# Sample's attention: one buffer of transposed rows with waits per piece, and five buffers of gathered rows instead of four

## The reference, cut to what matters

```python
def mla_sample(q_lat, q_pe, ckv_new, kpe_new, pool_ckv, pool_kpe, page_table):
    DB, T, H, C = q_lat.shape
    ckv_past = pool_ckv[page_table].reshape(DB, -1, KV_LORA)
    kpe_past = pool_kpe[page_table].reshape(DB, -1, MLA_ROPE)
    s_past = jnp.einsum('bqhc,bkc->bhqk', q_lat, ckv_past) + jnp.einsum('bqhr,bkr->bhqk', q_pe, kpe_past)
    ...
    p = jax.nn.softmax(s, axis=-1).astype(ckv_new.dtype)
    return (jnp.einsum('bhqk,bkc->bqhc', p[..., :P], ckv_past)
            + jnp.einsum('bhqk,bkc->bqhc', p[..., P:], ckv_new))
```

## Time and profile before

| what | value |
|---|---|
| median of three runs | 2132.25 us (2132.25 to 2144.01) |
| profiled execution | 2130.03 us, its span 2128.3 us |
| mean granted TensorE clock | 0.981 |
| PE, DVE, ACT, POOL busy in the span | 94%, 68%, 36%, 13% |
| the stage of the change | from 821.4 us (first transpose) to about 1341 us |

### The profile page before, as it was taken

The page is one execution under the profiler, slowest core; times in us unless marked ns, Lnnn a source line. Parts: engine busy times, 40 slices in busy tenths (PEclk is TensorE's granted clock), DMA queues, the critical chain, the costliest instruction groups (busy, mean ns, idle before and its releaser), DMA issues. The chain is left out here.

```text
span 2128.3 us, 46882 instructions
## 1 busy us (share of the span) xinstructions
PE 2001.5 (94%) x19749; PEld 1683.8 (79%) x19749; DVE 1444.2 (68%) x2515; ACT 761.8 (36%) x1488; POOL 280.5 (13%) x368
## 2 busy tenths in 40 slices
PE   7899999999999997999999899799899999999998
PEld 6899977799997785777777767667788888778886
DVE  3747655474865625998989998587677777655555
ACT  5433323342332211344334333544454444521110
POOL 1000001000001011322222322211410200000000
PEclk9999999999999998999999999899999999999999
DMA  7323345752337765999999999579938822344442
GB/s 244 113 90 108 120 149 174 236 187 84 98 119 224 258 245 237 394 382 364 381 356 388 371 375 338 187 295 385 303 72 143 144 43 102 135 156 164 148 148 89
DMA packets 194517, 454.78 MB, mean 214 GB/s; under 512 B 15072, under 2 KB 106240, under 8 KB 185104
## 3 DMA queue, kind: packets, MB, share of 16 engines
q0 software_dynamic: 53648, 252.12, 36.8%
q1 hardware_dynamic: 140672, 199.81, 27.9%
HBM read 350.00 MB, written 101.69 MB: 212 GB/s over the span
## 5 line engine op out<-in xcount | busy, mean ns | idle before, releaser
L2838 PE MATMUL sa_ps_s<-sa_turned,keep_q 128*32 128x128 f32 x5120 | 183.8, 278 | 37.3 <-DVE sa_turned L2594 31.4
L1178 PE MATMUL pj_ps<-pj_w,pj_xh_s 128*128 128x256 f32 (+1 forms) x1088 | 194.3, 282 | 0.0
L2838 PEld LDWEIGHTS sa_ps_s<-sa_turned,keep_q 128*32 128x32 f32 x5120 | 133.7, 111 | 64.7 <-DVE sa_turned L2594 43.1
L1178 PE MATMUL pj_ps<-pj_w,pj_xh 128*128 128x256 f32 (+1 forms) x960 | 173.9, 284 | 4.4 <-DVE pj_kT L873 4.4
L1178 PEld LDWEIGHTS pj_ps<-pj_w,pj_xh_s 128*128 128x128 f32 x1088 | 168.1, 190 | 0.3 <-issue 0.3
L2594 DVE STREAM_TRANSPOSE sa_turned<-sa_nat 128x2048 f32<-128x2048 f32 x64 | 146.9, 2295 | 21.5 <-DMA sa_kp<-cache_kpe,keep_index 21.5
L1178 PEld LDWEIGHTS pj_ps<-pj_w,pj_xh 128*128 128x128 f32 x960 | 150.2, 194 | 10.4 <-issue 10.4
L879 DVE TENSOR_TENSOR pj_w<-pj_raw,pj_w 128x1024 fp32r<-128x1024 f32 (+1 forms) x86 | 102.6, 1193 | 77.2 <-ACT pj_w L701 77.0
L2594 DVE STREAM_TRANSPOSE sa_turned<-keep_nat 128x2048 f32<-128x2048 f32 x64 | 146.7, 2292 | 9.7 <-PEq L85 4.9
L1178 PE MATMUL pj_ps<-pj_w,pj_xl_s 128*128 128x256 f32 (+1 forms) x544 | 153.1, 281 | 0.0
L701 ACT CAST pj_w<-pj_raw 128x1024 fp32r<-128x1024 f32 (+1 forms) x86 | 88.1, 1025 | 154.9 <-PE pj_ps L1178 84.4
(11 more groups left out here) (529 smaller groups left out, 5016.1 us busy)
## 6 DMA issues: line engine op xcount, KB each, us to landing
pj_raw<-w_in POOLq DMA_DIRECT2D x32, 1024.0 KB, 7.0
s_zn<-pj_c SPq DMA_DIRECT2D x32, 512.0 KB, 3.0
rm_z<-s_zn SPq DMA_DIRECT2D x16, 768.0 KB, 9.6
s_zt<-pj_c SPq DMA_DIRECT2D x20, 512.0 KB, 3.5
s_x<-pj_late_x SPq DMA_DIRECT2D x32, 256.0 KB, 3.7
s_k<-lp_st SPq DMA_DIRECT2D x16, 512.0 KB, 9.2
s_v<-lp_st SPq DMA_DIRECT2D x16, 512.0 KB, 5.1
s_qn<-lp_st SPq DMA_DIRECT2D x16, 512.0 KB, 9.7
```

What stands on the lines that cost most here:

```text
L1178: mm = pe.matmul(ps[:, bank + u, x2 * SW:x2 * SW + w], of[a][:, k, rows_at:rows_at + P], wt[:, b, k, 0:w], start=opens and (x2, k, a, b) = ...
L2838: mm = pe.matmul(ps_s[j * QR:(j + 1) * QR, s, 0:TQ * QR], q32[:, u, c, :], turned[:, s, c, j * TQ:(j + 1) * TQ, :].rearrange("p x q -> p ( ...
```

## The change

`DEEP` becomes 5, so there is a fifth `nat` and `kp` (20 KB per partition), and `turned` has one half instead of two (20 KB less). The gather of step g waits for the values of step g - 5. With one buffer of transposed rows, piece n of step g may be written when PE has read piece n of step g - 1: PE now signals after each piece (`piece_ps`, in place of `s_ps`), and every `turn(g, n)` with g of 1 or more waits for it. `new_low` waits for three pieces per step. The last steps that use buffers 0 and 1 (`last_use`) stay 60 and 61, and the waits of the loads for the next stage follow from them. `head_roots` moves by one gather in POOL's order.

```diff
--- before.py
+++ after.py
@@ -2376,7 +2376,7 @@
 PAGES_SEEN = GP // QUADS
 CH = (KVL + ROPE) // QR
 ROWS_Q = QUADS * HEADS
-DEEP = 4
+DEEP = 5
 STRIDE = STEPS // BLOCKS
 PIECES = ((0, 4), (4, 8), (8, 10))
 
@@ -2406,7 +2406,7 @@
         r.sems.extend([keep.rows_in, keep.rows1_in])
         nat = [keep.nat, keep.nat1] + [r.sb(f"nat{k}", [P, TPP, KVL]) for k in range(2, DEEP)]
         kp = [keep.kp, keep.kp1] + [r.sb(f"kp{k}", [P, TPP, ROPE]) for k in range(2, DEEP)]
-        turned = r.sb("turned", [P, 2, CH, TPP, QR])
+        turned = r.sb("turned", [P, CH, TPP, QR])
         none = r.sb("none", [P, TQ * QR])
         negated = r.sb("negated", [P, TQ * QR])
         ratio = r.sb("ratio", [P, 2])
@@ -2426,10 +2426,10 @@
         ps_s = r.ps("ps_s", [P, 2, 512])
         ps_p = r.ps("ps_p", [P, 512])
         ps_o = r.ps("ps_o", [P, 512])
-        (late_in, acc_clear, acc_in, chain, t_ok, s_ps, low_ok, exp_ok,
+        (late_in, acc_clear, acc_in, chain, t_ok, piece_ps, low_ok, exp_ok,
          p_ps, p_ok, pv_ps, acc_ok, fin_dve, fin_pe, fin_act, next_kv_in, next_k_in, next_q_in, next_w_in, square_ok, mean_ok,
          next_ok, w_hi) = [
-            r.sem(n) for n in ("late_in acc_clear acc_in chain t_ok s_ps low_ok exp_ok "
+            r.sem(n) for n in ("late_in acc_clear acc_in chain t_ok piece_ps low_ok exp_ok "
                                "p_ps p_ok pv_ps acc_ok fin_dve fin_pe fin_act next_kv_in next_k_in next_q_in next_w_in square_ok mean_ok "
                                "next_ok w_hi").split()]
         sums = r.sb("sums", [P, 2, BATCH4])
@@ -2479,6 +2479,10 @@
         cat_r_out, cat_m_out = m.sem("cat_r_out"), m.sem("cat_m_out")
         S_DEC = [float(np.float32((1.0 - 2.0 ** (-5.0 - h)) ** P)) for h in range(HEADS)]
 
+        def last_use(k):
+
+            return max(g for g in range(STEPS) if g % DEEP == k) + 1
+
         def begun(g, after):
 
             b, rest = divmod(g - 1 - after, STRIDE)
@@ -2506,8 +2510,8 @@
 
                 def load_next():
 
-                    sp.wait_ge(pv_ps, STEPS - DEEP + 1)
-                    sp.wait_ge(nat_in[(STEPS - 1) % DEEP], 32 * (STEPS // DEEP))
+                    sp.wait_ge(pv_ps, last_use(0))
+                    sp.wait_ge(nat_in[(STEPS - 1) % DEEP], 32 * ((STEPS - 1) // DEEP + 1))
                     rows = t["s_zn"][0:WIDE, O_CQ:NAT].rearrange("(x p) n -> p x n", p=P)
                     sp.dma_start(begin.latent[:, :, QL:], rows[:, :, QL:]).then_inc(next_kv_in, 16)
                     sp.dma_start(begin.gains[:, QL:], t["mla_kvnorm_g"].to_broadcast([P, KVL])).then_inc(next_kv_in, 16)
@@ -2568,8 +2572,8 @@
                         if g >= DEEP:
                             pool.wait_ge(pv_ps, g - DEEP + 1)
                         gather(pool, t, index, g, nat[g % DEEP], kp[g % DEEP], nat_in[g % DEEP])
-                    if begun(g - 2, 3) is not None:
-                        head_roots(begun(g - 2, 3))
+                    if begun(g - DEEP + 2, 3) is not None:
+                        head_roots(begun(g - DEEP + 2, 3))
 
                 for n, (a, w) in enumerate(((1, KVL), (0, QL))):
                     pool.wait_ge(square_ok, BATCH4 * (n + 1))
@@ -2581,22 +2585,22 @@
             def _(dve):
                 link = linker(dve, chain)
                 def turn(g, n):
-                    k, s = g % DEEP, g % 2
+                    k = g % DEEP
                     a, z = PIECES[n]
                     if n == 0:
                         if g == 0:
                             dve.wait_ge(keep.rows_in, 32)
                         else:
                             dve.wait_ge(nat_in[k], 32 * (g // DEEP + (k > 0)))
-                        if g >= 2:
-                            dve.wait_ge(s_ps, g - 1)
+                    if g >= 1:
+                        dve.wait_ge(piece_ps, len(PIECES) * (g - 1) + n + 1)
                     of = nat[k][:, :, a * QR:z * QR] if n < 2 else kp[k][:, :, :]
-                    dve.transpose(turned[:, s, a:z, :, :].rearrange("p c x q -> p x c q"),
+                    dve.transpose(turned[:, a:z, :, :].rearrange("p c x q -> p x c q"),
                                   of.rearrange("p x (c q) -> p x c q", q=QR)).then_inc(t_ok, 1)
 
                 def new_low(g):
                     u, s = g // PER_SET, g % 2
-                    dve.wait_ge(s_ps, g + 1)
+                    dve.wait_ge(piece_ps, len(PIECES) * (g + 1))
                     if g >= 1:
                         dve.wait_ge(low_ok, g)
                     dve.tensor_tensor_reduce(out=negated[:, :], in0=ps_s[:, s, 0:TQ * QR], in1=none[:, :], scale=-1.0,
@@ -2819,7 +2823,7 @@
                 act.wait_ge(fin_dve, 2)
                 act.activation(share[:, :, :], below[:, :, :], ACT.Exp, scale=1.0).then_inc(fin_act, 1)
                 act.wait_ge(next_k_in, 16)
-                act.wait_ge(pv_ps, STEPS - DEEP + 2)
+                act.wait_ge(pv_ps, last_use(1))
                 act.copy(begin.w_k[:, 0, :, :], begin.raw_k).then_inc(w_hi, 1)
                 act.wait_ge(late_in, 32)
                 act.copy(begin.w_v[:, 0, :, :], w_uv[:, :, :]).then_inc(w_hi, 1)
@@ -2836,10 +2840,9 @@
                     for c in range(a, z):
                         for j in range(QUADS):
                             mm = pe.matmul(ps_s[j * QR:(j + 1) * QR, s, 0:TQ * QR], q32[:, u, c, :],
-                                           turned[:, s, c, j * TQ:(j + 1) * TQ, :].rearrange("p x q -> p (x q)"),
+                                           turned[:, c, j * TQ:(j + 1) * TQ, :].rearrange("p x q -> p (x q)"),
                                            start=(c == 0), stop=(c == CH - 1))
-                    if n == len(PIECES) - 1:
-                        mm.then_inc(s_ps, 1)
+                    mm.then_inc(piece_ps, 1)
 
                 def pull_probs(g):
                     s = g % 2
```

## The result

The changed kernel takes 2144.46 us, median of 20 runs (2138.93 to 2151.05), against 2133.14 us (20 runs, 2125.57 to 2147.06) for the kernel before: 11.3 us more, ratio 1.0052, 95% interval 1.0038 to 1.0066. The forecast was 2122 us, with a range of 2108 to 2136. The profiled execution of after took 2151.05 us with a span of 2149.3 us, at the upper end of its runs, and before's 2130.03 us with 2128.3 at the middle of its own; of the 21.0 us between the two spans about half is scatter between runs, so sizes are taken from medians and only places from the traces.

The account below looks back on a forecast made before the run. In the attention stage DVE, PE and DMA were taken as nearly full, with 26.3 us of DVE's waits for rows removable. Fifth buffer 10 us gained, one transposed buffer 0, the rest 0: 2122 us, range 2108 to 2136.

Parts of the forecast that it names:

- What bounds the kernel now: Sample's attention: DVE, PE and DMA nearly full; DVE's 26.3 us of waits for rows are all a deeper ring can remove.
- What moves beside it: Head norm roots, loads for the next stage and memory: the shifts around the change cost 0.
- subtracted 2.8 us: DVE's waits before 951 us, taken off the gain: DMA engines 0.99 busy, so one more queued gather adds nothing.
- The fifth buffer: Gathers in the attention stage: one more always queued, so DVE waits less for rows; 10 us gained.
- the term of 11.6 us: Fourteen DVE waits for rows outside step 4b+2, where DVE's own work fills the step: 11.6 us, counted in full.
- the 10 us made from it: Gain taken for the fifth buffer: 11.6 us after subtractions, DMA room of 12 to 13 us, some waits remaining.
- 4.1 us in seven waits: Step 4b+2: PE covers about 1.0 us of each of twelve waits; 4.1 us beyond cover counted as gain.
- One buffer for transposed rows: New wait before each transpose for the same piece of the step before: cost 0, bounded by 5 us.
- Rival 1: DMA engines at their ceiling, gathers land later and DVE waits as before: 0 to 4 us gained, 2131; chance 0.19.
- Rival 2: PE reaches step 4b+2 earlier, so the 10.5 us counted as covered are gained too: likely 20 us, 2110; chance 0.13.
- Rival 3: Fuller gather queue delays PE's instruction refills: at 0.25 us each, 10 us slower, 2142; chance 0.09.
- what the profile after would show: Waits for rows under 10 us, all before 950 us; 380 GB/s or more after 951; longer PE waits; stage about 510 us.

Follow-up runs that it names:

- experiment 2: One buffer for transposed rows with waits by piece, but four buffers for gathered rows, against the kernel before: 2133.48 us, ratio 0.9998.
- the mended kernel: The changed kernel with the retention's gain load issued early by ScalarE instead of late on SyncE's list, against the kernel before: 2133.77 us, ratio 0.9992.
- experiment 1: Gain load issued early by ScalarE: in the changed kernel 2133.77 us (0.9992), in the kernel before 2132.88 us (0.9999), both against the kernel before.

## Why the prediction was wrong

**What bounds the kernel now** read DVE's waits for rows and the DMA share rightly, but took DVE's waits for rows for the thing to remove, and did not ask which loads of the start land just in time. The 0.60 us of ACT at 865.21 us were in the trace and in none of the groups.

**What moves beside it** is the step that failed and made the sign wrong. It put at 0 everything but the gathers themselves, and the fifth buffer's part spoke of "one more gather issued at once" only as a gain. That gather and the standing backlog behind it take DMA time from SyncE's twelve loads of the start. Measured: gain load 12.2 us later to land (47.2 against 35.0), 10.7 us between the medians with and without the cause. The part on the fifth buffer subtracted 2.8 us because the DMA engines were 0.99 busy in the first window; that row should have been read the other way as well: where the engines are full, a transfer issued earlier delays another.

**The fifth buffer**: the waits went as forecast, the price put on them was wrong. DVE's waits for rows fell to 0.5 us (forecast: under 10) and DVE's waits for PE rose. But the term of 11.6 us for the fourteen waits that "count in full" was no gain, nor were the 10 us made from it: with the start mended the fifth buffer gives 2133.77 against 2132.88 us. PE, not DVE, ended most of these steps as soon as rows came in time: between steps 7 and 62 DVE is idle for 45.9 us with five buffers, 44.8 of them for PE, and for 41.0 with four, 19.4 for rows and 20.3 for PE. The prediction compared positions inside one trace, where PE was itself held back by the same late rows; that this is why it took PE's time for cover in one position and for nothing in the others is argued. Its 4.1 us in seven waits also come out as 4.5 us in eight with a cover of 1.0 us, which changes nothing.

**One buffer for transposed rows**: 0 was right (experiment 2). With five buffers ten of its new waits bind, 6.7 us together, with no loss that the five-buffer kernels show against the kernel before.

**Rival 1, the DMA ceiling**, with its 2131 us would have come within 3 us of the mended kernel, by luck: the waits for rows did not stay, which was its mechanism. **Rival 2** fell, since no gain came. **Rival 3** named the right direction, slower, and a real mechanism: PE waits at fixed places for its instructions, and these gaps are gone without rows. But this is not what made the kernel slower: with the gain load early the gaps are there and the time is level. They take back a part of what the fifth buffer gives (5.6 of 7.6 us in the one pair of traces). Of **what the profile after would show**, the waits for rows came true (the one left lies before 950 us), as did DVE's longer waits for PE; the 380 GB/s (349 to 366) and the stage of 510 us (540) did not, and the landing of gathers can't be read from the trace after.

## What to carry to other kernels

Before a queue of transfers is made deeper, list the small loads that share the DMA engines with it and look how long before their first use each lands; a load that is waited for at all, if only for 0.6 us, has nothing to spare. Issue such loads ahead of the bulk or on a queue with nothing in front (5.3 us instead of 35 to 47). And a wait for data that hides behind full DMA engines is worth only what the next engine leaves: take the data away altogether in one run (here 27 to 30 us) and then the wait alone (here 0) before a buffer is spent on it. Look in that run's trace, too, for what the omission changes elsewhere (here 5 to 7 us behind the stage). No version here that reads all its rows beats the kernel before clear of noise.

## What the runs showed of the hardware

A 2 KB load in 4-byte elements took 5.2 or 5.3 us with nothing ahead of it on its queue, 33 to 35 us behind some 2.1 MB not yet landed there, and 46 or 47 us when gathers were always pending beside it. PE lost 22 to 27 us between steps 7 and 62 in gaps of over 0.9 us on the grid with all rows at a DMA share of 0.95 to 0.97 (before, after, and the two of experiment 1), 5.9 us at 0.63, 1.1 us at 0.18, and 56 us at 0.99 with 1 KB pieces. Of the gaps on the grid 243 of 247 ended 2.0 to 2.7 us after a 16 KB transfer of the instruction queue began. After the stall at step 6, in which PE had been idle for 10.3 us, the block's first four matmuls took 1.08 us where the same four take 0.66 in the trace before. The granted clock was 0.50 from 879 to 882 us (1.2 instead of 2.4 GHz); over the window of 97.5 us the clock was 0.95 instead of 1.00.
